# Load schedule of the modulation vector's weight rows in a one-core kernel of a mixed MLA / expert / SSM block: four buffers to the end of the expert stage, one request every four tiles

## What is computed

```python
def peer_ffn(h, w_pq, peer_keys, peer_u, peer_v):
    ...
        u = jnp.take(peer_u, i_blk, axis=0)
        a = jax.nn.gelu(jnp.einsum("td,thkd->thk", x_blk, u)) * g_blk
        v = jnp.take(peer_v, i_blk, axis=0)
        return jnp.einsum("thk,thkd->td", a, v)
...
        x = x + peer_ffn(h2, w_peer_q[l], peer_keys[l], peer_u[l], peer_v[l])
    return rmsnorm(x, g_final)

def second_block(x, c, positions, w_mod, b_mod, ...):
        mod = jax.nn.silu(c) @ w_mod[l] + b_mod[l]
        sh1, sc1, g1, sh2, sc2, g2 = jnp.split(mod, N_MOD, axis=-1)
        h = rms_norm(x, norm1_g[l]) * (1.0 + sc1[:, None]) + sh1[:, None]
```

## Time and profile before

| | |
|---|---|
| median of three runs | 3476.58 us (3474.68 to 3477.68) |
| the profiled execution's own time | 3481.2 us |
| its span, first to last instruction | 3479.6 us |
| TensorE matmul busy | 3465.7 us |
| VectorE busy | 2642.4 us |
| ScalarE busy | 1920.5 us |
| GpSimd busy | 155.0 us |
| DMA | 859.68 MB, mean 247 GB/s |
| main loop of the expert stage | about 1276 to 1622 us of the span |
| pairs, with the last one | about 1622 to 2159 us |

### The profile page before, as it was taken

The page is one execution under the profiler, slowest core; times in us unless marked ns, Lnnn a source line. Parts: engine busy times, 40 slices in busy tenths (PEclk is TensorE's granted clock), DMA queues, the critical chain, the costliest instruction groups (busy, mean ns, idle before and its releaser), DMA issues.

```text
span 3479.6 us, 47171 instructions
## 1 busy us (share of the span) xinstructions
PE 3465.7 (100%) x16466; PEld 2891.3 (83%) x16466; DVE 2642.4 (76%) x3560; ACT 1920.5 (55%) x2476; POOL 155.0 (4%) x213
## 2 busy tenths in 40 slices
PE   9999999999999999999999999999999999999999
PEld 8888888888888888888788888888888888888888
DVE  6664567679888878887888888899976666666668
ACT  6555444545588864444444445657755555545544
POOL 3100000000000000000000000110000000000000
PEclk9999999999999999999999999999999999999999
DMA  8556668976667799999999997665557677777774
GB/s 296 178 161 205 190 195 288 301 226 216 218 221 260 257 324 361 324 328 281 354 342 331 342 341 251 195 183 175 170 178 253 210 217 214 234 229 213 232 231 159
DMA packets 333136, 859.68 MB, mean 247 GB/s; under 512 B 146800, under 2 KB 147696, under 8 KB 318624
## 3 DMA queue, kind: packets, MB, share of 16 engines
q1 hardware_dynamic: 260752, 663.31, 60.2%
q10 hardware_dynamic: 54784, 112.80, 9.6%
q0 software_dynamic: 17424, 81.23, 6.4%
HBM read 773.72 MB, written 52.45 MB: 237 GB/s over the span
## 4 chain that ended last, share of the span: by engine, by line
PE 96%; issue 1%; DVE 1%; DMA 1%; ACT 0%; ACTq 0%; SPq 0%; POOL 0%; POOLq 0%; DVEq 0%
PE ps L2847 29%; PE ps L2848 29%; PE ps L2849 29%; PE ps L2958 1%; PE ps L2960 1%; PE ps L2959 1%; PE ps L3223 1%; PE ps L3505 1%; DMA mraw<-in_w_mod 1%; PE ps L3509 0%; DMA act_scratch<-UB 0%; PE ps L2975 0%; DVE lo L1644 0%; PE ps L2906 0%; PE ps L3352 0%
## 5 line engine op out<-in xcount | busy, mean ns | idle before, releaser
L869 ACT CAST hi<-raw 128x1024 fp32r<-128x1024 f32 (+1 forms) x1214 | 1274.4, 1052 | 1395.2 <-PE ps L2849 1275.2
L1644 DVE TENSOR_TENSOR lo<-raw,hi 128x1024 fp32r<-128x1024 f32 (+1 forms) x1212 | 1467.8, 1219 | 742.6 <-ACT hi L869 740.1
L2847 PE MATMUL ps<-hi,xx 128*128 128x512 f32 x2752 | 1080.7, 393 | 0.0
L2848 PE MATMUL ps<-lo,xx 128*128 128x512 f32 x2752 | 1072.0, 390 | 0.0
L2849 PE MATMUL ps<-hi,xx 128*128 128x512 f32 x2752 | 1071.5, 389 | 0.0
L2847 PEld LDWEIGHTS ps<-hi,xx 128*128 128x128 f32 x2752 | 517.0, 188 | 111.2 <-issue 4.2
L2849 PEld LDWEIGHTS ps<-hi,xx 128*128 128x128 f32 x2752 | 516.6, 188 | 108.7
L2848 PEld LDWEIGHTS ps<-lo,xx 128*128 128x128 f32 x2752 | 517.1, 188 | 103.0
L2847 PE MATMUL ps<-hi,Ph 128*128 128x512 f32 x1020 | 398.4, 391 | 5.2 <-DVE lo L1644 5.2
L2849 PE MATMUL ps<-hi,Pl 128*128 128x512 f32 x1020 | 397.6, 390 | 0.0
L2848 PE MATMUL ps<-lo,Ph 128*128 128x512 f32 x1020 | 397.5, 390 | 0.0
(11 more groups left out here) (542 smaller groups left out, 3772.8 us busy)
## 6 DMA issues: line engine op xcount, KB each, us to landing
raw<-in_peer_u SPq DMA_DIRECT2D x256, 512.0 KB, 4.4
raw<-in_peer_v SPq DMA_DIRECT2D x256, 512.0 KB, 6.7
mraw<-in_w_mod ACTq DMA_DIRECT2D x96, 1024.0 KB, 7.8
raw<-in_w_up SPq DMA_DIRECT2D x176, 512.0 KB, 4.2
raw<-in_w_in SPq DMA_DIRECT2D x143, 512.0 KB, 3.7
raw<-in_in SPq DMA_DIRECT2D x128, 512.0 KB, 3.7
raw<-in_w_down SPq DMA_DIRECT2D x88, 512.0 KB, 4.5
raw<-in_out SPq DMA_DIRECT2D x64, 512.0 KB, 4.3
```

What stands on the lines that cost most here:

```text
L869: SC.copy(hi[:, n0 % SPL, 0:w], raw[:, n0 % RAW, 0:w]).then_inc(hi_ready, 1)
L1644: V.tensor_tensor(lo[:, n0 % SPL, 0:w], raw[:, n0 % RAW, 0:w], hi[:, n0 % SPL, 0:w].bitcast(F32), ALU.subtract).then_inc(lo_ready, 1)
L2847: PE_.matmul(acc, xhi[:, k0 + k, xs], H, start=s0, stop=False)
L2848: PE_.matmul(acc, xhi[:, k0 + k, xs], L, start=False, stop=False)
```

## The change

The units of the pairs use all four slots, except the last two (46 and 47 of 48), which go to slots 0 and 1 as before. ScalarE asks for four units before the main loop; from then on it asks for one unit every four tiles, behind the tiles n+7, n+11, n+15 and n+19 of every step and pair, each for the slot whose unit was four before it. The last pass of the main loop asks for the first four units of the pairs. The order of VectorE's units is the same; only the slot and the count in their waits differ. The load of `gfin` moves on GpSimd's queue behind all loads of gates, and waits for 44 of the 48 late units in place of the end of the main loop.

```diff
+LATE = 2 * AHEAD
+
+
+def late_slot(u):
+    return u % 4 if u < LATE - 2 else u % 2
+
...
-            pool.wait_ge(mod_used, PARTS * KD)
-            pool.dma_start(gfin[:], A["g_final"].partition_broadcast(P)).then_inc(gains_in, 16)
             for v in range(MAIN + 1, NBLK):
                 gates_in(v, v % 2)
+            pool.wait_ge(mod_used, PARTS * KD + LATE - 4)
+            pool.dma_start(gfin[:], A["g_final"].partition_broadcast(P)).then_inc(gains_in, 16)
...
-            def mod_load(u, rr):
+            def mod_next(u, rr):
+                act.wait_ge(mod_used, rr * KD + (u - 3))
                 act.dma_start(mraw[:, u % 4], A["w_mod"][bass.ds(rr * KD + u, 1)].rearrange("a p n -> p (a n)")
                               ).then_inc(mod_in[u % 4], 16)
...
             act.wait_ge(g_st[1], 32)
+            for u in range(4):
+                act.dma_start(mraw[:, u], A["w_mod"][u]).then_inc(mod_in[u], 16)
             with act.Fori(0, MAIN // 4) as rr:
-                act.wait_ge(mod_used, rr * KD)
-                for u in range(2):
-                    mod_load(u, rr)
                 for i in range(4):
-                    n, off = n0 + 16 * i, rr * 64
-                    for j in range(4):
-                        split(n + 4 + 2 * j, off)
-                        split(n + 5 + 2 * j, off)
-                        u = 4 * i + j
-                        if u + 2 < KD:
-                            act.wait_ge(mod_used, rr * KD + u)
-                            mod_load(u + 2, rr)
+                    n, off, u = n0 + 16 * i, rr * 64, 4 * i + 4
+                    for j in range(4, 12):
+                        split(n + j, off)
+                        if j in (7, 11):
+                            mod_next(u + j // 4 - 1, rr)
...
                     for j in range(14, 20):
                         split(n + j, off)
+                        if j in (15, 19):
+                            mod_next(u + j // 4 - 1, rr)
...
             def mod_fetch(u):
-                act.wait_ge(mod_used, PARTS * KD + max(u - 1, 0))
-                act.dma_start(mraw[:, u % 2], A["w_mod"][PARTS * KD + u]).then_inc(mod_in[u % 2], 16)
+                s = late_slot(u)
+                act.wait_ge(mod_used, PARTS * KD + (u - 3 if s == u % 4 else u - 1))
+                act.dma_start(mraw[:, s], A["w_mod"][PARTS * KD + u]).then_inc(mod_in[s], 16)
...
-                    elif p in (4, 6, 10, 12):
-                        mod_fetch(u + 2 + (4, 6, 10, 12).index(p))
-
-            mod_fetch(0)
-            mod_fetch(1)
+                    elif p % 4 == 3 and u + 4 + p // 4 < LATE - 2:
+                        mod_fetch(u + 4 + p // 4)
+
...
             def mod_late(u):
-                row, part = mraw[:, u % 2], PARTS + u // KD
-                dve.wait_ge(mod_in[u % 2], 64 * PARTS + 16 * (u // 2 + 1))
+                s = late_slot(u)
+                row, part = mraw[:, s], PARTS + u // KD
+                dve.wait_ge(mod_in[s], 64 * PARTS + 16 * (u // 4 + (1 if s == u % 4 else 2)))
```

## The result

The changed kernel is slower: its median is 3494.83 us (3480.53 to 3507.36, 11 executions), that of the kernel before on the same chip 3474.68 us (3473.18 to 3486.47, 11 executions). The ratio is 1.0042 with the interval 1.0025 to 1.0060. The forecast was 3471.5 us; the sign is that of rival D, which had 0.07, and even its 3484.0 us is 11 short.

What follows compares the result with a forecast made beforehand. TensorE was taken as the bound, with one event of 7.44 us to win and all other terms nothing; 5.1 us, the middle of 2.8 and 7.44, off the median 3476.58 gave 3471.5 us, range 3468.5 to 3477.5.

Steps and rivals of the forecast that it cites:

- rival D: Pairs: requests 1.2 to 2.6 us behind transposes cause two TensorE stalls of 7.4 us; slower, 3484.0 us, chance 0.07.
- the later transposes: Pairs: a unit 1.2 us behind a transpose makes 7.2 us about 9.6 to 11.8; tiles have 18 us: nothing.
- The start of the main loop: Four units at once before the loop delay weight tiles: nothing, or at most about 1 us.
- The unit of the first pair: Its third unit, asked for earlier, lands by 1631.7, wanted at 1647.2; VectorE's wait goes, with 15 us to spare.
- forecast 8 to 14: Landing time in us expected for the first pair's long transpose, which took 25.2 us before.
- old jam: First pair: a 25.2 us transpose with late unit and weight tile; fewer bytes around it were expected to shorten it.
- The price of the event: First pair: TensorE loses 5.37 us waiting and 2.07 us at slow clock, 7.44 us, all taken as gone.
- `gfin` late: Last part: the moved load has 31 us before its first user at 2127.9 us; costs nothing.
- Carrying it to the timed runs: Called the weak step: of 7.44 us won in the profiled execution, 5.1 us were taken for the timed median.
- the two cases that were averaged: Timed runs lose the full 7.44 us (3469.1 us), or only 2.8 us (3473.8 us).
- The signs: If right: no TensorE wait above 1.3 us, no lower clock in 1600 to 2100, no `mraw` wait in the pairs.
- C: Rival: a jam as large comes elsewhere, at the burst or a transpose; 7.44 us lost and won, 3476.6 us, chance 0.11.

Runs made afterwards that it cites:

- e1: The changed kernel with the pairs' requests moved back to the places of before (p = 4, 6, 10, 12): 3484.48 us, ratio 1.0016.
- e2: The changed kernel with the pairs' requests one tile later (p = 4, 8, 12 and 0 of the next pair): 3496.67 us, ratio 1.0052.
- e3: The changed kernel with the pairs' requests two tiles later (p = 5, 9, 13 and 1 of the next pair): 3483.25 us, ratio 1.0012.
- e12: e13 with each pair's first request behind p = 3 in place of p = 4: 3506.62 us, ratio 1.0084.
- e16: e12 once more, unchanged, on another chip: 3495.53 us, ratio 1.0052.
- e11: e13 with each pair's fourth request behind p = 15 in place of p = 12: 3525.15 us, ratio 1.0132.
- e10: e13 with four units at once, in place of two, at the start of each pass of the main loop: 3474.35 us, ratio 0.9985.
- e6: The changed kernel without 44 of the 48 unit loads of the pairs, so with wrong rows there: 3486.87 us, ratio 1.0011.
- e14: e1 with two units before the main loop and the next two behind n+5 and n+7 of the first step: 3488.35 us, ratio 1.0055.
- e5: The kernel before with only the `gfin` load moved late, as in the change: 3474.38 us, ratio 0.9982.
- e13: The same kernel as e5 (kernel before, only `gfin` late) on another chip: 3475.14 us, ratio 0.9992.
- e9: The changed kernel with two units before the main loop, later first-step requests respaced, one extra first-pair unit, pairs' places as in the change: 3481.06 us, ratio 0.9999.
- e7: All 80 units asked for on SyncE's queue between its tile loads, four slots, 12 tiles ahead of use: 3476.84 us, ratio 0.9979 to the kernel before.

## Why the prediction was wrong

**The step that failed** is the one on the later transposes: "Price by the rows: 7.2 becomes about the 9.6 to 11.8 us of the others, 2 to 5 us on tiles that have 18 us. Nothing, with 6 us of cover left". Measured: 18.2 us in the median and 28.7 at most for 20 of them, and tiles landing after 22 us. The price was taken from rows in which a unit stands 4.8 us behind a transpose or 7 us ahead, and carried to 1.2 us. The steps between show that the price is anything but flat: median landings of 7.5 us with the units 7 us ahead of the first transpose and 4.8 behind the second (e1), 12.6 and 12.9 where the second has one 3 to 4 us ahead too (e2, e3), 14.0 and 15.7 with one 2.6 behind the second (e12, e16), 18.2 with one 1.2 behind the first (e11) and in the change, which has one 2.5 behind the second too. The trace of before had no row at 1.2 us. Its nearest one spoke for the prediction, and the prediction doesn't list it: the transpose of 1619.6, with two units asked for 2.4 and 2.8 us behind it,

```profile
L576 SPq DMA_TRANSPOSE AT<-act_scratch x1: 4985/4985/4985, 1619.6 to 1619.6; - x1
...
DMA to landing us min/median/max: 10.6/10.6/10.6
```

(in e1 the same one, with a unit 2.4 us behind, takes 9.6, in the change 12.8). So closeness alone doesn't always do it; why this one is spared is not shown. The row that warned was the 25.2 us transpose, with units 4.4 and 9.9 us behind, and the prediction read it as a jam of bytes that fewer bytes would cure.

**Rival D** had the mechanism in the right words and 0.07. Its two stalls of 7.4 us are not what came: in the profiled execution 20 stretched transposes gave six small stalls in the pairs, without lower clock; its sum is low by 11 us against the median. It also didn't see the second place, the start of the main loop.

**The start of the main loop** was costed at "Nothing, or at most about 1 us", with the burst as the danger. Alone the burst is harmless (e10); with the change's rhythm behind it the profile has 1.66 us at 1313, about that size. The cost lay in what the prediction didn't list: the new rhythm puts a unit 2.9 us ahead and one 6.3 behind the transpose at 1312, which had none beside it, and its landing goes from 10.8 to 19.3 us (27 to 28 in e1, e6 and e14). Where that is the only part left it costs 9 to 12 us in the median (e1, e6).

**The unit of the first pair**: right. It was in time, and VectorE never waits for `mraw` in the pairs. The first pair's second transpose lands in 14.5 us, just outside the forecast 8 to 14. But four slots weren't needed for it: with `gfin` gone from 1605 the two old slots and the old places do as well (e5). That this load's leaving 1605 would ease the old jam was mentioned and given no price of its own; by e5 and e13 it is enough by itself. The price of the event, 7.44 us, was right: without it the profiled executions are 7.2 and 7.8 us lower.

**`gfin` late costs nothing**: right (28.3 us of wait on GpSimd, nobody behind it; e5).

**Carrying it to the timed runs**: the profiled execution of before was not the common one. In e5 and e13 the whole event is gone, and the median against that of before is 7.5 us lower on one chip and 0.4 higher on the other, while the fastest executions agree. So an event of the size of the earlier trace rows seems to be in a part of the executions only (the others were not profiled): of those of before between 2 in 11 and 18 in 35 are above 3480, by the chip. Neither of the two cases that were averaged, all or a fixed part, is so.

**The signs** that were named did their work: waits over 1.3 us near 1300 and at other transposes were named for C or D; the sign for slow clock in 1600 to 2100 is absent in the profiled execution and there in e9.

What stays open: why a unit on another queue stretches a transpose so far (pieces of a quarter didn't cure it); why the transpose of the first step with a unit 6.4 us behind is hit, and the later ones with 7.8 are not; and where the longest executions of the change lose their time.

The version to keep is the kernel before with `gfin` late, with or without the burst (e5, e13, e10): 3474.4 to 3475.1 us, with 1 of 36 executions above 3480. The kernel before has medians of 3474.7 to 3481.9 by the chip, so what is won is the steadiness; a lower median is shown on one chip only. It takes nothing of the change but the move that was costed at nothing.

## What to carry to other kernels

A load on another queue that is asked for within one to three microseconds behind a DMA transpose can make it two to four times as long, and everything behind it on its queue with it: place such loads so that the last one ahead of a transpose is some 7 us ahead and the next one at least 5 us behind (e1), or give them to the transpose's own queue (e7), and where a trace has a transpose of 25 us among those of 7, look first at what is asked for around it, a single broadcast load 25 us ahead included. A price read from rows at one distance doesn't hold at another when requests move against each other. And where the profiled execution is above the median, one stall in it may be in few executions: look at the spread of times before pricing it.

## What the runs showed of the hardware

- At a DMA share of 1.17 to 1.24 the engines moved 72 to 97 GB/s during a stretched transpose, and 385 to 415 in undisturbed windows of the same kernels. A high share says nothing of what is moved.
- SyncE was held for 20.8 us by asking for one transpose (4.7 to 6.8 us for the 18 of the kernel before), so that its queue stood empty behind it.
- The same distance on another queue and on its own: a unit 0.9 to 1.0 us ahead of a transpose on ScalarE's queue, 16.9 to 17.6 us to landing (the change); one 0.7 to 0.9 us ahead on SyncE's, 7.5 to 11.0 us (e7).
- With the same order of requests the effect varies from execution to execution: e12 and e16, one kernel, had medians of 3506.6 and 3495.5 us; the change ranges over 27 us, e10 over 2.
- Gaps of TensorE up to 1.7 us left the granted clock at 1.00 (changed kernel, 1600 to 2100 us); those of 4.5 and 6.7 us (e9, e1) were followed by matmuls 0.43 us apart and a granted clock of 0.57 and 0.74 in their windows, the lower level of 1.2 GHz for a part of them.
